# Grid items threaded between dense and dilated items, merges in the transposing banks: a two-layer hybrid-attention encoder

## What is computed

```python
for l in range(DEPTH):                                  # 2 layers
    o_a = dense_attention(qa, ka, va)                   # 6 heads, 1024 x 1024 scores
    o_b = dilated_sliding_attention(q, k, v)            # 6 heads, as one masked 1024 x 1024 softmax
    o_c = neighbourhood_attention(q, k, v, rpb[l])      # 4 heads; 128 queries see 12 x 32 keys
    mixed = concat([rms_norm(o_a), rms_norm(o_b), rms_norm(o_c)])
    x = x + mixed @ w_out[l]
    x = x + square(relu(rms_norm(x) @ w_mlp_in[l])) @ w_mlp_out[l]
```

## Time and profile before

| what | value |
|---|---|
| median of 3 runs | 2977.53 us (2973.89 to 2981.43) |
| profiled execution | 2986.88 us, span 2985.1 us |
| PE busy | 2872.7 us (96%) |
| DVE, ACT busy | 1753.1 us (59%), 1057.6 us (35%) |
| mean granted PE clock | 0.985 |

### The profile page before, as it was taken

How to read it: one execution, slowest core, us unless ns; L and a number is a source line. 1 busy time by engine, 2 the same in 40 slices (tenths; PEclk the granted TensorE clock), 3 DMA queues, 4 the chain that set the end, 5 groups by cost and what they waited for, 6 DMA issues and landing times.

```text
span 2985.1 us, 39896 instructions
## 1 busy us (share of the span) xinstructions
PE 2872.7 (96%) x14640; PEld 2450.0 (82%) x14640; DVE 1753.1 (59%) x3038; ACT 1057.6 (35%) x1992; POOL 92.0 (3%) x69
## 2 busy tenths in 40 slices
PE   7999899998999999999998989999899999999998
PEld 7998778887888888888798977788788888888887
DVE  5642787885554555455666337878755555455457
ACT  5332666774311111111234235678732111111113
POOL 0000210000000000000000011200000000000000
PEclk9999999999999999999999999999999999999999
DMA  5656755413111111111146576543130111111111
GB/s 192 184 180 171 173 145 119 97 39 120 43 43 42 56 42 56 42 42 63 49 174 197 168 188 153 145 94 93 48 113 29 57 42 56 42 42 56 42 61 68
DMA packets 194007, 281.11 MB, mean 94 GB/s; under 512 B 47184, under 2 KB 153296, under 8 KB 184144
## 3 DMA queue, kind: packets, MB, share of 16 engines
q1 hardware_dynamic: 190032, 262.56, 30.6%
q0 software_dynamic: 3840, 16.78, 1.5%
HBM read 208.50 MB, written 70.78 MB: 94 GB/s over the span
## 4 chain that ended last, share of the span: by engine, by line
PE 82%; DVE 7%; issue 3%; DMA 3%; ACT 2%; DVEq 1%; SPq 1%; ACTq 0%; POOL 0%; POOLq 0%
PE ps L1356 23%; PE ps L1181 20%; PE ps L1371 18%; PE ps L1254 6%; PE ps L1271 5%; PE ps L1300 5%; PE ps L1311 2%; PE ps L1149 1%; DVE prob L1001 1%; DMA biasC<-in_bias_c 1%; PE ps L1218 1%; DVE x L1102 1%; DVE pT L831 1%; DMA values<-vst 1%; DVE hn L848 1%
## 5 line engine op out<-in xcount | busy, mean ns | idle before, releaser
L1371 PE MATMUL ps<-w_dn,hid 128*128 128x512 f32 x3072 | 712.9, 391 | 1.4
L1356 PE MATMUL ps<-hT,w_up 128*128 128x512 f32 x3072 | 702.5, 390 | 3.3 <-DVE hT L831 3.3
L1371 PEld LDWEIGHTS ps<-w_dn,hid 128*128 128x128 f32 x3072 | 573.8, 188 | 131.7 <-DVE x L1102 14.1
L1356 PEld LDWEIGHTS ps<-hT,w_up 128*128 128x128 f32 x3072 | 576.4, 188 | 122.9 <-ACT rbuf L781 3.7
L1181 PE MATMUL ps<-ws,hT 128*128 128x384 f32 (+3 forms) x3072 | 606.4, 356 | 2.7 <-issue 1.6
L1181 PEld LDWEIGHTS ps<-ws,hT 128*128 128x128 f32 x3072 | 535.6, 190 | 48.2 <-issue 2.4
L1102 DVE TENSOR_TENSOR x<-ps,x 128x512 f32<-128x512 f32 x512 | 342.7, 689 | 223.6 <-PE ps L1371 223.4
L718 ACT ACTIVATE pT<-ps 128x512 fp32r<-128x512 f32 (+1 forms) x448 | 240.6, 581 | 190.4 <-PE ps L1271 187.3
L1089 DVE TENSOR_TENSOR vbuf<-rbuf 128x512 f32<-128x512 f32 x128 | 88.6, 692 | 371.0 <-ACT rbuf L781 371.0
L831 DVE TENSOR_TENSOR pT<-ps,pT 128x512 fp32r<-128x512 f32 (+1 forms) x448 | 281.5, 664 | 13.8 <-ACT pT L718 13.8
L781 ACT ACTIVATE rbuf<-ps 128x512 f32<-128x512 f32 x128 | 76.6, 598 | 553.9 <-PE ps L1356 553.9
(11 more groups left out here) (84 smaller groups left out, 2142.8 us busy)
## 6 DMA issues: line engine op xcount, KB each, us to landing
raw<-in_wstream SPq DMA_DIRECT2D x76, 1024.0 KB, 4.9
head<-feats SPq DMA_DIRECT2D x192, 256.0 KB, 6.1
feats<-tst SPq DMA_DIRECT2D x128, 192.0 KB, 2.5
values<-vst POOLq DMA_DIRECT2D x32, 384.0 KB, 3.1
head<-values SPq DMA_DIRECT2D x24, 512.0 KB, 4.0
biasC<-in_bias_c SPq DMA_DIRECT2D x16, 768.0 KB, 7.7
raw<-in_wstream SPq DMA_DIRECT2D x12, 768.0 KB, 6.0
x_park<-x SPq DMA_DIRECT2D x16, 512.0 KB, 9.3
```

The lines of the kernel that those rows point to most:

```text
L1356: last = pe.matmul(ps[:, k % 2, :], w_up[0 if first else 1][:, w1, kt, ft * P:(ft + 1) * P], hT[:, w2, kt, sh * 512:(sh + 1) * 512], start ...
L1371: last = pe.matmul(ps[:, 2 + m % 4, :], hid[slot][:, w1, ft, s * P:(s + 1) * P], w_dn[1 if last_group else 0][:, w2, ft, nh * 512:(nh + 1) ...
```

## The change

**Order.** The items of A and B heads run on as one line, A heads first. After the fifth of them and then after every second one a C item is set in, 8 times, then there is a gap; this repeats every 24 A or B items. So the C heads 0, 1, 2 and 3 lie among A and B items, and the last A or B items follow without C items.

**Blocks.** A block of a C head is now 2 items (one column block of the grid, upper and lower half), weighed in one step into its own layout; `O` keeps it in that order. The normalization's transposes put the tokens back in place (`grid_tokens`). A sum's reciprocal is applied where the merged block is moved to `O`, for C as for the others; the scaling of C probabilities is gone.

**Merges.** `merge(b)` writes into bank 4 or 5, in one sequence `TSEQ` with the transposes. It waits (`t_free`) until the user of the bank two places before it is through.

**Bias.** Four tables per C head of half the size, used as they are: DVE takes a maximum and negates it in a small instruction of its own. POOL negates nothing.

**Loads and output.** C queries, keys and values have their own buffers, in the room of `raw`; the weights of "o0" are loaded after the last C block is weighed. The projection "o0" takes tiles 0 to 3 over 6 of 8 row blocks, then the last 2 row blocks (which hold the C heads, and need all four tiles), then the same for tiles 4 to 7.

```diff
+HEADS = [("A", h_) for h_ in range(HA)] + [("B", HA + h_) for h_ in range(HB)]
+GRID_LEAD, GRID_STEP, GRID_PERIOD = 4, 2, 24
+for j_ in range(8 * NAB):
+    ITEMS.append((*HEADS[j_ // 8], j_ % 8))
+    k_, r_ = divmod(j_ - GRID_LEAD, GRID_PERIOD)
+    if 0 <= k_ < HC and r_ % GRID_STEP == 0 and r_ < 8 * GRID_STEP:
+        ITEMS.append(("C", HA + HB + k_, r_ // GRID_STEP))
...
+for n_, (kind_, h_, q_) in enumerate(ITEMS):
+    per_ = 2 if kind_ == "C" else 4
+    if q_ % per_ == per_ - 1:
+        BLOCKS.append((n_ + (3 if kind_ == "C" else 6), kind_, h_, q_ - per_ + 1, per_))
...
+for b_, (f_, kind_, _, _, _) in enumerate(BLOCKS):
+    for part_ in range(4):
+        WEIGH_AT[f_ - (0 if kind_ == "C" else 3 - part_)].append((b_, part_))
...
+for n_ in range(STEPS):
+    if 2 <= n_ < NI + 2:
+        TSEQ += [("turn", g_) for g_ in ITEM_GROUPS[n_ - 2]]
+    TSEQ += [("merge", b_) for b_ in blocks_at(n_ - 2)]
+def t_bank(what, n):
+    return 4 + TSEQ.index((what, n)) % 2
...
+                def t_free(what, n):
+                    at = TSEQ.index((what, n))
+                    if at >= 2:
+                        before, m = TSEQ[at - 2]
+                        if before == "turn":
+                            pe.wait_ge(t_lo, l * NGR + m + 1)
+                        else:
+                            pe.wait_ge(o_ready, l * NB + m + 1)
...
                 def merge(b):
+                    t_free("merge", b)
                     pe.wait_ge(ot_ready, l * NB + b + 1)
...
-                        dve.tensor_scalar(prob[:, it % 2, 0:CW], prob[:, it % 2, 0:CW], a_rd[:, it:it + 1], None,
-                                          ALU.mult).then_inc(pn_ready, 1)
...
-                    pool.tensor_scalar(bias, bias, -1.0, None, ALU.mult).then_inc(biasc_neg, 1)
...
+                            dve.drain()
+                            dve.tensor_scalar(a_nm[:, col:col + 1], a_mx[:, col:col + 1], -1.0, None, ALU.mult)\
                                .then_inc(mx_ready, 1)
...
-                    if t >= 3:
-                        residual(l, acc + t - 3, 0, t - 3)
+                    if t >= 5:
+                        residual(l, acc + t - 5, 0, t - 5)
                     if t in (5, 6):
                         split_job(l, "o1", t - 5)
...
-                for s in range(ST):
+                for s in range(4):
                     pe.wait_ge(nt_free, l * TN + 2 * (ST + s + 1) + 2)
+                    project(l, acc + s, "o0", s, (0, 6))
+                    if s < 3:
                         norm_turn(l, ST, s + 2)
+                for s in range(4):
+                    project(l, acc + s, "o0", s, (6, 8))
+                    if s < 3:
+                        norm_turn(l, ST, s + 5)
```

More of the change, by code:

```diff
@@ new lines, in load_values, with load_grid @@
+                sp.dma_start(words(head[k][:, 4096:5120]).rearrange("p (t d) -> p t d", d=P),
+                             values[:, h * P:(h + 1) * P].rearrange("(t p) d -> p t d", p=P))\
+                  .then_inc(value_in[k], 16)
+            def load_grid(l, k):
+                if k:
+                    sp.wait_ge(s_done, l * NI + grid_item(8 * k - 1) + 1)
+                gb = words(grid_qk[:, :])
+                fq, fk = F_CQ + k * HD, F_CK + k * HD
+                for part in range(2):
+                    rows = slice(64 * part, 64 * part + 64)
+                    sp.dma_start(gb[rows, 0:1024], feats[part, fq:fq + HD, :]).then_inc(grid_in, 16)
+                    for w in range(2):
+                        sp.dma_start(gb[rows, 1024 * (1 + w):1024 * (2 + w)], feats[w, fk:fk + HD, :])\
+                          .then_inc(grid_in, 16)
@@ L471, in _ @@
                         first_head(l, e[2], turn, vt)
-                    if e[0] == "split":
+                    if e[0] == "split" and e[1] != "cv":
                         u = unit_of(e[1], e[2]) + 2
@@ L508, in _ @@
                 hold(sp)
-                for n in range(1, NH):
-                    if n == 1:
-                        stores_done(l)
-                        sp.dma_start(tabB[:, :], bias_b).then_inc(tab_in, 16)
-                    load_head(l, n)
+                stores_done(l)
+                sp.dma_start(tabB[:, :], bias_b).then_inc(tab_in, 16)
+                load_grid(l, 0)
+                load_bias(l, 0)
+                load_features(l, 1)
+                load_grid_values(l, 0)
+                load_bias(l, 1)
+                load_values(l, 1)
+                for _, what, n in LOADS:
+                    if what == "features":
+                        load_features(l, n)
+                    elif what == "values":
+                        load_values(l, n)
+                    elif what == "grid":
+                        load_grid(l, n)
+                    elif what == "grid values":
+                        load_grid_values(l, n)
+                    elif what == "bias":
+                        load_bias(l, n)
+                    else:
+                        sp.wait_ge(pv_done, l * NB + C_ORDER[-1] + 1)
+                        load_unit(l, unit_of("o0", n))
                 for t in range(ST):
@@ L971, in _ @@
                         turn += 1
-                for i in range(NI + 12):
+                for i in range(STEPS):
                     if i < NI:
@@ L1013, in _ @@
-                    if i >= 12 and (i - 12) % 4 == 0 and merged((i - 12) // 4):
-                        b = (i - 12) // 4
-                        kind, h, q = ITEMS[4 * b]
+                            nk, _ = group_keys(g)
+                            rest(turned(g, LO),
+                                 ps[:, t_bank("turn", g), 0:nk * P].rearrange("p (k s) -> p k s", s=P),
+                                 turned(g, HI)).then_inc(t_lo, 1)
+                    for b in blocks_at(i - 2):
+                        _, kind, h, q, per = BLOCKS[b]
@@ L1246, in scores @@
                     else:
+                        hb = head[HEADS.index((kind, h)) % 2]
                         for kh in range(2):
@@ L1402, with prob_before @@
 TST_BEFORE = [stores_before(n % NTS, n) for n in range(len(STORED))]
[L1403 to L1404 removed]
+HEAD_DMAS = {"A": 6 + 4, "B": 6}
 HEAD_N = [sum(HEAD_DMAS[kd] for kd, _ in HEADS[k::2]) for k in range(2)]
[L1406 to L1416 removed]
+def prob_before(b):
+    order, keep = (C_ORDER, 1) if BLOCKS[b][1] == "C" else (AB_ORDER, 2)
+    at = order.index(b) - keep
+    return order[at] if at >= 0 else -1
 def turn_of(stg):
```

367 lines of the change are left out of this document (189 added, 178 removed).

## The result

The changed kernel takes 3117.19 us (median of 4 runs, 3106.66 to 3131.7), the kernel before 2979.43 us in the same session: a ratio of 1.047, 95% interval 1.042 to 1.052. It is slower by 138 us, inside the range of 3035 to 3125 us, and above the 3065 to 3110 us of the case that the prediction held likeliest. The profiled execution took 3131.7 us, the slowest of the four, so its rows show some 14 us more than the median. The four executions differ in the clock: 3106.66 us at a mean granted clock of 0.973, 3131.7 us at 0.966.

What follows compares the result with a forecast made beforehand. PE was taken to bound both attentions. Per layer -18.0 + 3.3 + 13.9 + 30.6 + 9 + 16.5 = +55.3 us, +110.6 for two layers, on a 2977.53 us median: 3088 us, range 3035 to 3125.

Steps and rivals of the forecast that it cites:

- the case that the prediction held likeliest: Whole kernel: the forecast with all its terms, 3088 us, own range 3065 to 3110 us, chance 0.56.
- merge's bank: waits and the clock they cost: Both attentions: per layer 13.9 and 30.6 us of PE waits at merges, plus 9 us of lower clock.
- residual ahead of the scaling: Output projection: DVE adds residuals before scaling tile 5, so PE idles at tiles 5 to 7; +16.5 us per layer.
- the rest: scaling, negation, start, C group's low part: Attention: scaling and negation gone, -18.0 us per layer; later start at the first C item, net +3.3.
- The waits at the merge: Attention: 23 merges per layer wait for ACT's copy and DVE's subtraction to free their bank; 13.9 + 30.6 us.
- The 13.9 and 30.6 us: Merge waits per layer: eleven of 1.15 or 1.35 us among A and B items, twelve of 2.55 with C scores.
- The clock: Attention: clock falls after half of twelve long merge gaps per layer, 1.5 us each time; 9 us per layer.
- the clock falls after nearly every grid merge: Rival, chance 0.20: the alike gaps lower the clock almost always, 9 to 10 us more per layer; 3110 to 3130 us.
- the 18 us per layer: Attention clock loss the prediction would have put by the skill's section, instead of the 9 us it kept.
- The output projection: Behind attention: 12.5 us of PE idling at tiles 5 to 7 and some 4 us of clock; +16.5 us per layer.
- What the change takes away: Attention: 9.9 us of waits for scaled probabilities and up to 8.1 us of clock go; -18.0 us per layer.
- the first C features: Attention start: PE waits for their load, 9.0 us in the second layer, taken as 6 in the first.

Runs made afterwards that it cites:

- e1: Changed kernel with merges back in their block's own bank and transposes alternating between banks 4 and 5 as before; 3008.89 us, 1.009 times before.
- e4: Changed kernel with merges in the block's own bank and the residuals done late, both together; 2974.32 us, 0.998 times before.
- e6: Changed kernel with GRID_LEAD 5 instead of 4, so each C item stands one A or B item later; 3065.7 us, 1.029 times before.
- e7b: Changed kernel with one needless matmul (128x512, or two of 128x256 for a C block) ahead of the merge's wait; 3079.45 us, 1.034 times before.
- e5: Changed kernel with the merge issued behind the weighing of its step instead of ahead of it; 3040.05 us, 1.021 times before.
- e3: Changed kernel with DVE's first residual moved behind the scaling of tile 7 and the others behind the norm; 3087.2 us, 1.036 times before.
- e10: Kernel before without POOL's negation of the bias tables, DVE negating one column instead; scaling, order and banks kept; 2955.71 us, 0.992 times before.

## Why the prediction was right in direction and low in size

Its sum was +110.6 us; +137.8 was measured. Both, split as the experiments split them:

| part, both layers | predicted | measured | by |
|---|---|---|---|
| merge's bank: waits and the clock they cost | 70.2 + 18 = 88.2 | 108.3 | changed kernel less e1 |
| residual ahead of the scaling | 33.0 | 34.6 | e1 less e4 |
| the rest: scaling, negation, start, C group's low part | -29.4 + 18.8 = -10.6 | -5.1 | e4 less before |
| sum | 110.6 | 137.8 | |

The 18.8 us for the C group's low part are taken out of the predicted 2 x 44.5 = 89 of the first row and put into the last, where e1 shows that they belong. The last row also holds the split of the projection, some 8 us, which the prediction had at nothing.

- **The waits at the merge** were right in place, number and releaser: 23 per layer, behind DVE's low part. Their size was right too. The profile has 39.2 us per layer at both lines against 44.5, but the prediction counted from where PE could have started the merge, 0.88 us after the start of the transposes, and so included the 0.16 us on top: 39.2 + 37 x 0.16 = 45.1 us. Counted like this, a step that scores a C item has 0.66 + 1.33 to 0.82 + 1.38 us and 0.32, so 2.3 to 2.5 against 2.55; those among A and B items have 1.20 to 1.40 against 1.15 to 1.35. The 13.9 and 30.6 us stand.
- **The clock is the term that was too low:** "If the clock falls after half of them and costs 1.5 us each time". In the profiled execution it falls after 12 of 12 per layer, and by e1 it costs some 21 us per layer, 1.7 each. The price was near; the number of falls was put at half of what it is. That is the rival "the clock falls after nearly every grid merge", which had 0.20 and its 3110 to 3130 us hold the result. The row that I rested on showed one long wait of 2.91 us; that two waits of 0.8 and 1.4 us with four transposes between them do the same was not in any row of before. The section of the Trainium skill that I had set against it ("TensorE: Matmul & The Clock Gate", "A second HAM failure mode: psum-queue depth-cycling") states no size; the 18 us per layer that I would have put by it were my own figure, and nearer than my 9. The trace agrees with what it describes, brief idle times with the clock swinging between two levels: 0.92 to 0.93 granted in attention, against 0.98 without the waits at the merge. e6, e7b and e5 show the cause three ways: by moving the merge to another step, by filling the gap, by shortening it.
- **The output projection** was predicted at 16.5 us per layer; the profile shows 20.7, of which e3 gives back 17.1 and the split projection keeps 3.6. The waits were 5.67, 5.67 and 3.55 us instead of 4.9, 4.9 and 2.7. I left out that the transposes of tile 5 also wait for the low part of tile 4, which DVE does behind the scaling.
- **What the change takes away** was -18.0 per layer. e10 gets 11.3 per layer from the negation alone with the scaling in place. The -5.1 us of the last row show that interleaving gives most of this back: 9.4 us per layer at L1372, which I had charged to the merge's wait, some 4 for the split projection, and 5.3 us for the first C features in the changed kernel (7.3 in e4), against a predicted mean of 7.5.

The result lies in the upper part of the range. The term for the clock was argued from a single row of before and came out at less than half of what was measured; the range held the result because the rival on the clock had been put into it. The 24 of 24 are read from one execution of the changed kernel; that the idle time is the cause is shown by e7b. Part of the clock loss changes from run to run: the changed kernel's four executions spread over 25 us with clocks of 0.966 to 0.973, and e3's trace shows 19 of 24.

## What to carry to other kernels

A result that must be put into a ring of two banks waits for the slowest user of that ring; ask whose read frees the bank, and what is queued behind on the engine that waits. Price a wait on PE at its own length only if it stands alone: two short ones in a step with little work cost clock as well, here some 42 us beside 67 us for all waits at the merge, and then moving one of them by a step, or putting work that is due anyway into it, gives more back than the wait's own length. Before an engine gets an idle neighbour's work, look at what that does to the operations it runs beside: here the kernel without a negation on the idle POOL was 22 us faster, while the reordering with both of its costs taken out gave 5.

## What I had not expected of the hardware

- Needless matmuls made the kernel faster: 3079.45 against 3117.19 us with 27 of them per layer. The mean clock of the whole execution was 0.984 against 0.966 in the two profiles.
- A DVE operation of 0.42 us lasted up to 3.81 us when it started while POOL's ran, and in no place more than 0.43 without it.
- The lower clock followed 24 of 24 merges with a pair of waits of some 0.7 and 1.35 us in one execution and 19 of 24 in another with the same waits; behind a single wait of 1.04 to 1.24 us in the kernel before with a shared bank it followed 2 of 36. With the C items one place later it followed one of 12 pairs of 0.54 and 1.09 us.
